# Seven block products for eight in the projections of a recurrent layer and a gated delta layer

## The reference, cut to what matters

```python
def rglru_block(h, in_w, ...):                       # layer 1
    proj = h @ in_w                                  # 1024x1024 @ 1024x2048
    xb, zg = proj[..., :D_RNN], proj[..., D_RNN:]
    xb = causal_dwconv(xb, conv_w) + conv_b
    gates = sigmoid(xb per block @ gate_w + gate_b)
    a_t, b_t from the gates; hseq = scan(a_t, b_t)
    return (hseq * silu(zg)) @ out_w

def gated_deltanet_block(h, in_w, ...):              # layer 2
    proj = h @ in_w                                  # q, k, v, z: 4 x 1024 columns, and 16 more
    qkv = silu(causal_dwconv(proj[..., :o1], conv_w))
    q, k normalised; chunked gated delta rule per head, 8 heads of 128
    return (rms-normed o * silu(z)) @ out_w

x = x + gate * out                                   # after each of the two
```

## Time and profile before

| | |
|---|---|
| median of 3 runs | 2334.98 us (2333.48 to 2340.04) |
| the profiled execution | 2349.8 us |
| its span, first to last instruction | 2348.1 us |
| mean granted TensorE clock | 0.988 |
| PE busy | 2269.5 us, 97% |
| DVE busy | 1205.7 us, 51% |
| ACT busy | 542.0 us, 23% |
| POOL busy | 95.9 us, 4% |

### The profile page before, as it was taken

One profiled execution on the slowest core, in us unless ns is written; L12 is line 12 of the kernel. 1 busy time (PEld: TensorE's weight loads), 2 busy tenths in 40 slices (PEclk: granted clock), 3 DMA queues, 4 the chain that ended last, 5 costly groups with the idle time before them and its releaser, 6 DMA issues. The chain is left out here.

```text
span 2348.1 us, 20195 instructions
## 1 busy us (share of the span) xinstructions
PE 2269.5 (97%) x7290; PEld 1159.0 (49%) x7290; DVE 1205.7 (51%) x1712; ACT 542.0 (23%) x860; POOL 95.9 (4%) x79
## 2 busy tenths in 40 slices
PE   6999999999999999999999998999999999999999
PEld 5444444346656556556554454544444444444443
DVE  4666533253563653644722587347469998341112
ACT  4334422222332332332312510031100000230011
POOL 0000000110101101101010000000000000000000
PEclk8999999999999999999999999899999999999999
DMA  8332310021101101101120224231111111115001
GB/s 313 109 131 86 110 46 0 1 52 45 34 20 40 42 20 40 42 18 43 47 37 18 100 55 73 54 93 33 41 40 41 36 32 45 31 41 188 18 27 45
DMA packets 197709, 134.28 MB, mean 57 GB/s; under 512 B 49868, under 2 KB 171777, under 8 KB 197633
## 3 DMA queue, kind: packets, MB, share of 16 engines
q1 hardware_dynamic: 187825, 131.82, 19.5%
q10 hardware_dynamic: 9440, 0.59, 0.3%
q0 software_dynamic: 384, 1.05, 0.2%
HBM read 118.06 MB, written 14.19 MB: 56 GB/s over the span
## 5 line engine op out<-in xcount | busy, mean ns | idle before, releaser
L1701 PE MATMUL bank<-hT,ring 128*128 128x512 f32 x1472 | 637.3, 594 | 2.6 <-DMA ring<-in_w_in 2.6
L986 PE MATMUL bank<-hT,ring 128*128 128x512 f32 x992 | 461.4, 594 | 0.0
L1701 PEld LDWEIGHTS bank<-hT,ring 128*128 128x128 f32 x1472 | 280.1, 191 | 352.5 <-issue 349.0
L2319 DVE SCALAR_TENSOR_TENSOR yT<-s_arena,yT 128x1024 f32<-128x1024 f32 x240 | 308.3, 1285 | 8.4
L986 PEld LDWEIGHTS bank<-hT,ring 128*128 128x128 f32 x992 | 172.5, 191 | 136.0 <-issue 136.0
L478 PE MATMUL bank<-hT,ring 128*128 128x512 f32 x448 | 194.9, 593 | 0.0
L478 PEld LDWEIGHTS bank<-hT,ring 128*128 128x128 f32 x448 | 85.0, 190 | 105.0 <-issue 104.6
L1701 PE MATMUL bank<-yT,ring 128*128 128x512 f32 x256 | 110.0, 593 | 0.0
L1929 PE MATMUL bank<-resid,s_arena 128*128 128x512 f32 x256 | 110.0, 593 | 0.0
L1437 DVE SCALAR_TENSOR_TENSOR memory<-memory,col_exp_last,bank 128x128 f32<-128x128 f32 x64 | 22.3, 348 | 162.5 <-PE bank L1109 162.5
L1701 PE MATMUL bank<-ssm_y,ring 128*128 128x512 f32 x192 | 83.9, 593 | 0.6 <-DVE s_arena L2333 0.6
(11 more groups left out here) (449 smaller groups left out, 2621.4 us busy)
## 6 DMA issues: line engine op xcount, KB each, us to landing
ring<-in_w_in SPq DMA_DIRECT2D x48, 512.0 KB, 3.9
ada<-in_ada_w SPq DMA_DIRECT2D x8, 2048.0 KB, 7.9
ring<-in_gdn_in_w SPq DMA_DIRECT2D x32, 512.0 KB, 4.8
ring<-in_lru_in_w SPq DMA_DIRECT2D x16, 512.0 KB, 7.0
lru_arena<-in_ada_w SPq DMA_DIRECT2D x6, 1024.0 KB, 12.9
resid<-in_x SPq DMA_DIRECT2D x4, 1024.0 KB, 8.2
decayT<-g_scratch SPq DMA_DIRECT2D x8, 512.0 KB, 4.2
x_scratch<-resid SPq DMA_DIRECT2D x8, 512.0 KB, 6.4
```

The lines of the kernel that those rows point to most:

```text
L986: last = nc.tensor.matmul(bank[:, 2 * (b % 2) + n, :], ring[:, b, k, :], hT[:, k, n * HALF:(n + 1) * HALF], start=(k == 0), stop=(k == KT ...
L1701: last = nc.tensor.matmul(bank[:, 2 * PAIR[name] + h, :], w[:, k, :], src[:, k, h * HALF:(h + 1) * HALF], start=(k == 0), stop=(k == kt - 1))
L2319: dve_b.mark(dve.scalar_tensor_tensor(out=yT[:, n, :], in0=padded[:, p, j:j + S], scalar=taps[:, p, j:j + 1], in1=yT[:, n, :], op0=ALU.mul ...
```

## The change

A product of 2x2 blocks is made with seven block products for eight (the form of Strassen's method by Winograd). The "columns" of the block matrix are the two halves of k, the "rows" are a pair of weight tiles (x and z of a column in the recurrent layer; q with k, and v with z, in the delta layer), and the tokens are cut in two halves of 512. A block product is 4 matmuls of 128x512.

- **Sums of tokens**: T1, T2, T3 (128x2048 each) are made once per layer by DVE and kept in `resid`; T4 takes the place of a quarter of `hT`.
- **Sums of weights**: S1 to S4 (128x512 each) for every pair. In the recurrent layer DVE makes them, one column ahead; in the delta layer POOL does, those of pair b (v, z) behind `rel`, those of pair a (q, k) behind the level masks.
- **Products** are accumulated in two PSUM banks one upon another: P1, P1+P6, then P7 and P4 on top. Between them ACT keeps a copy of the partial sum (`keep`, 128x512 from PSUM to `resid`), and DVE adds it to a bank later (`part`, `join`).
- In the recurrent layer this holds for columns 2 to 7; columns 0 and 1 stay. z is now gated with one function (Silu) in two halves on ACT, and the weighing of a chunk of `ada_w` comes one column later. The order within a column is new on PE, ACT and DVE. x is loaded again into `resid` (4 x 1 MB) before it is added.
- In the delta layer it holds for the projections of heads 1 to 7; head 0 stays. The residual is stored to DRAM at the start of the stage (2 x 2 MB) and loaded again in the last head, between the loads of `out_w`. PE draws 56 instead of 64 in a head: 13 for 15 behind `v_flip`, and none behind `new` in chunks 2 to 7.

```diff
+                    for n in range(FAST, KT):
+                        if n > FAST:
+                            dve_a.wait(pe, f"C11_{n - 1}")
+                        product(n, 1, "A12", B21, f"x{n}", True, True)
+                        gates(n - 1)
+                        dve_a.wait(pe, f"S1_{n}")
...
+                        product(n, 2, "S1", T1, f"P5_{n}", True)
+                        dve_a.wait(pe, f"S2_{n}")
+                        act_a.wait(pe, f"kept0_{n}")
+                        product(n, sums_bank(n), "S2", T2, f"P6_{n}")
+                        dve_a.wait(pe, f"S4_{n}")
+                        act_a.wait(pe, f"kept2_{n}")
+                        product(n, 2, "S4", B22, f"P3_{n}", last_one=True)
+                        act_a.wait(pe, f"kept1_{n}")
+                        product(n, sums_bank(n), "S3", T3, f"P7_{n}")
+                        for j in weighed_in[n]:
                             later(j, n)
+                        if n < KT - 1:
+                            begin_column(n + 1)
+                        dve_a.wait(pe, f"C22_{n}")
+                        product(n, sums_bank(n), "A22", T4, f"z{n}", last_one=True)
+                    gates(KT - 1)
```

The same pair of products in the delta layer, on PE (pair a; pair b is alike, and its P1 and P2 come before a's P4):

```diff
+                        yield from product("a", 0, "A11", tok11, "P1", first=True)
+                        px_dve.wait(pe, "C11b", h, back=1)
+                        yield from product("a", 1, "A12", tok21, "P2", first=True, only=True)
...
+                        yield from product("a", 2, "S1", tok_sum1, "P5", first=True)
+                        sums["a"].wait(pe, "S2", h)
+                        tok_sums.wait(pe, "T2")
+                        px_act.wait(pe, "kept0a", h)
+                        yield from product("a", 0, "S2", tok_sum2, "P6")
+                        sums["a"].wait(pe, "S4", h)
+                        px_act.wait(pe, "kept2a", h)
+                        yield from product("a", 2, "S4", tok22, "P3")
+                        px_act.wait(pe, "kept1a", h)
+                        yield from product("a", 0, "S3", tok_sum3, "P7")
...
+                        px_dve.wait(pe, "C22a", h)
+                        tok_sums.wait(pe, "T4")
+                        yield from product("a", 0, "A22", tok_sum4, "P4")
...
-                        fill(15, 30)
+                        fill(13, 30)
...
-                            fill(1, 2)
+                            fill(int(c < 2), 2)
```

On ACT, POOL and DVE of the delta layer:

```diff
+                        if after is not None:
+                            keep(0, "a", h, "P1", "C11")
                         hd_pe.wait(act, "k_flip", h)
...
                         hd_act.mark(act.activation(cq[:, :], cq[:, :], ACT.Silu), "q_silu")
+                        if after is not None:
+                            keep(2, "a", h, "P5", "C22")
+                            keep(1, "a", h, "P6", "C12")
+                            px_act.mark(act.activation(padded[:, 0, PAD:PAD + HALF], bank[:, 1, :], ACT.Copy), "raw")
                         hd_pe.wait(act, "q_flip", h)
...
                             key_silu(after)
-                            take_z(after)
+                            hd_dve.wait(act, "y", h)
+                            px_dve.wait(act, "C22b", h)
+                            px_act.mark(act.activation(silu_z[:, HALF:S], z_raw, ACT.Silu), "zhi")
+                            px_pe.wait(act, "P4b", h)
+                            px_act.mark(act.activation(silu_z[:, 0:HALF], bank[:, 3, :], ACT.Silu), "zlo")
...
+                        done.mark(g.tensor_tensor(w["S3"], w["A11"], w["S1"], ALU.subtract), "S3")
+                        done.mark(g.tensor_tensor(w["S1"], w["S1"], w["A22"], ALU.add), "S1")
+                        done.wait(g, "S1", head - 1)
+                        done.mark(g.tensor_tensor(w["S2"], w["S1"], w["A11"], ALU.subtract), "S2")
+                        done.wait(g, "S2", head - 1)
+                        done.mark(g.tensor_tensor(w["S4"], w["A12"], w["S2"], ALU.subtract), "S4")
...
                         if after is not None:
+                            px_act.wait(dve, "zhi", h, back=1)
+                            join("C22b", z_raw, 3, 2, "P7b", h)
+                            join("C12b", padded[:, 2, PAD + HALF:], 2, 1, "P3b", h)
                             tap(after, 1, 0, "k", ck)
```

And on SP, in the last head:

```diff
                     sp.dma_start(out_w1, out_w[:, 0:7, HALF:D]).then_inc(out_loaded[2], 16)
+                    px_dve.wait(sp, "C12b", HEADS - 2)
+                    for n in range(2):
+                        sp.dma_start(resid[:, 4 * n:4 * n + 4, :], x1_dram[:, 4 * n:4 * n + 4, :]).then_inc(x1_back, 16)
                     sp.dma_start(ring_flat[:, 6 * HALF:8 * HALF], out_w[:, 7, :]).then_inc(out_loaded[3], 16)
```

More of the change, by code:

```diff
@@ new lines, in _, with product @@
+                    for j in weighed_in[0]:
+                        later(j, 1)
+                    dve_a.wait(pe, "sz0")
+                    pe_a.mark(project_column(1, 1), "z1")
+                    def product(n, to, w, v, name, first=False, last_one=False):
+                        w = blocks(n)[w]
+                        for k in range(KB):
+                            last = nc.tensor.matmul(bank[:, to, :], w[:, k, :], v[:, k, :], start=(first and k == 0), stop=(k == KB - 1), skip_group_check=not (first and last_one))
+                        pe_a.mark(last, name)
@@ new lines, in part @@
+                    def part(name, n, out, to, which, product):
+                        pe_a.wait(dve, f"{product}{n}")
+                        act_a.wait(dve, f"kept{which}_{n}")
+                        dve_a.mark(dve.tensor_tensor(out, bank[:, to, :], kept[which], ALU.add), f"{name}_{n}")
+                    for j in range(TAPS4):
+                        tap(0, j)
+                    weigh_later(0)
+                    gate_plain(0)
+                    weigh_later(1)
+                    gate_input(0)
@@ new lines, in _ @@
+                    gate_mult(0)
+                    recur(0)
+                    for j in range(TAPS4):
+                        tap(1, j)
+                    finish(0)
+                    finish(1)
+                    dve_a.mark(dve.tensor_tensor(T1, T4, B11, ALU.subtract), "T1")
+                    dve_a.mark(dve.tensor_tensor(T3, B22, T4, ALU.subtract), "T3")
+                    gate_plain(1)
+                    dve_a.wait(dve, "T1")
+                    dve_a.mark(dve.tensor_tensor(T2, B22, T1, ALU.subtract), "T2")
```

343 lines of the change are left out of this document (285 added, 58 removed).

## The result

The changed kernel takes 2342.07 us, the median of 16 runs (2336.63 to 2349.78). The kernel before, run beside it, takes 2336.4 (16 runs, 2332.63 to 2341.89). The ratio is 1.0026 with a 95% interval of 1.0015 to 1.0037: a loss of 5.7 us, where a gain of 7.3 was forecast, and 0.07 us above the range. Its profiled execution took 2345.05 us (span 2343.3).

What follows compares the result with a forecast made beforehand. PE, busy 2269.5 of 2348.1 us, was taken as the bound, though delta-head fillers sit in others' waits. Recurrent -19.5 and delta +12.2 gave -7.3, so 2327.5 us against the median of 2334.98; range 2308 to 2342.

Steps and rivals of the forecast that it cites:

- Recurrent layer, -19.5: Columns 2 to 7: 28 matmuls for 32 take 20.6 us off PE, nearly all kept; bounds -20.6 and -12.
- Where PE would stand: Delta heads: PE waits 3.0 us before P3 of pair a and 1.6 before the last product; v_flip 2.5 late.
- The sum of an undisturbed head, +0.9: One delta head: Y16 +1.0, chunks -1.4, end +1.3, so nothing of 6.9 us saved comes through; bounds -0.8 and +4.5.
- the 1.1 taken in all: Delta head: DVE loses 1.1 us beside POOL's sums: 0.3 at a small product, little at decay_a, 0.8 at q's taps.
- Head 0, +1: Start of the delta layer: T4, 2.7 us of DVE ahead of head 0's rel, partly shows, costing 1 us.
- The clock, +0.7 a head: Delta heads: PE's clock falls behind the 3.0 us wait, taken as three in ten of 2.4 us; ends 0 and 2.4.
- the 2.60 us without loss: Profile row: behind a PE wait of 2.60 us, 32 records took 14.00 us, as in 13.90, so no clock loss.
- the 12.2 forecast: Delta layer's total cost: 7 x (0.9 for the head + 0.7 for the clock) + 1 for head 0 = +12.2 us.
- 0.24 us won for a filler of 0.858: Chunks 2 to 7 of a delta head: mem still needs ACT's scaling, so each chunk gains only 0.24; six times, -1.4.
- no contention: Rival, delta heads: POOL and DVE don't meet on the path, wait near 2 us, clock never falls; 2315 us; chance 0.26.
- The clock falling in every head: Rival, delta heads: the clock falls each time behind the wait on kept2a, 7 x 1.7 us more; 2339 us; chance 0.20.
- The others: Rivals: clock falls in the chunks, 2399 us (0.07); PE's work alone counts, 2266 (0.05); last head's reload late, 2333 (0.04).

Runs made afterwards that it cites:

- the run of that part alone: Kernel before with only the recurrent layer's part of the change, delta layer as before: 2318.46 us, 18.1 below the kernel before.
- both_waits: Changed kernel with ACT's copy kept2a ahead of q_silu and DVE's additions C12b and C22b inside chunks 5 and 7: 2327.15 us.
- keep_early: Changed kernel with one edit: ACT makes the copy kept2a ahead of q_silu instead of behind it: 2336.28 us.
- pool_late: Changed kernel with one edit: POOL makes pair b's four sums of weights behind the second level mask instead of behind rel: 2328.53 us.
- delta_alone: Kernel before with only the delta layer's part of the change, recurrent layer as before: 2358.89 us, 22.3 above the kernel before.
- joins_in_chunks: Changed kernel with one edit: DVE makes additions C12b and C22b behind delta of chunks 5 and 7, not behind the last chunk: 2335.46 us.
- fill_behind_new: Changed kernel with one edit: in chunks 2 to 7 the one filling matmul is drawn behind new instead of ahead of it: 2320.26 us.
- three_edits: Changed kernel with the edits of keep_early, joins_in_chunks and pool_late together: 2315.60 us.
- four_edits: three_edits with, at the delta heads' start, PE's wait for head 0's z moved to before P5 and DVE's T4 made earlier: 2316.13 us.

## Why the prediction was wrong

Told by its own steps:

- **Recurrent layer, -19.5.** Right: 19.1 in the traces, 18.1 by the run of that part alone. No wait over 1 us on PE in columns 2 to 7.
- **Where PE would stand.** Right: 3.05 us before P3 of pair a (3.0 forecast), 1.47 before the last product (1.6), `v_flip` 2.7 late (2.5), no fall of the clock in the chunks, and a head longer and not shorter by 8 fewer fillers.
- **The sum of an undisturbed head, +0.9.** Too low: it is +1.5 (94.92 less the 1.3 by which `Y16` came later behind the fall at 590 is 93.6, for 92.12). `Y16` is 1.31 late (704.01 - 668.32 = 35.69 for 34.38), not 1.0, because POOL costs DVE 1.4 at two small operations, where I had put 0.3 at one, and 0.1 at `decay_a`, for the 1.1 taken in all; at the taps, where I had put 0.8, it costs nothing outside the first head, since POOL's last sum ends at 677.87, as they begin. So 1.5 for 1.1 is near by luck: it fell on other operations than those named. The chunks bring 0.14 each and not 0.24, so -0.8 for -1.4, and the end costs 1.0 for 1.3. That is 0.6 too little in each of seven heads, 4.2 us. This is the first term of the sum that failed.
- **Head 0, +1.** Too low, and with the wrong cause; this is the largest step that failed. By the part run alone, from PE's first matmul of the delta layer to the first `k_flip` are 61.61 us (412.73 to 474.34) and 63.63 with the change (412.31 to 475.94): +2.0, of it 1.76 a wait for ACT's gating of z that I hadn't listed. And the head behind it takes 3.8 more than an undisturbed one, by T4 and POOL's sums in each other's way and a wait of 4.57 with its fall of the clock. I had let T4 act on that head's `rel` only, as part of the 1. In both_waits, where the clock doesn't fall there, the first head is 1.7 over the others, so of the 3.8 about half is the clock (an estimate).
- **The clock, +0.7 a head.** The term was a little low (5.5 us over the last six heads, for 4.2 by 0.7 each), and half its mechanism was missing: I took falls behind the wait of 3.0 only, and three of the six came behind the wait of 1.47, which I took to be inside another delay and free. I had read from the 2.60 us without loss that a shorter wait is safe; that row follows a stretch of nothing but 128x512 products, and the wait of 1.47 follows eight chunks of small ones. The first heads show that the row wasn't a limit elsewhere either: the clock fell behind a wait of 2.54 us in keep_early. All this is of one traced execution for each kernel; how often the clock falls in the other executions of the median isn't known.

So the delta layer costs 21.9 in the traces for the 12.2 forecast: 4.2 in the sum of a head, 4.8 at the first head and ahead of it, the rest in the clock. With 1.4 less from the recurrent layer in the medians that is most of the 13 us between -7.3 and +5.7. Of the rivals, no contention is refuted by pool_late. The clock falling in every head, with 2339 us, is what came nearest: it fell in six of seven, if not always where that rival said. I had given it 0.20. Its number is near by luck, since it put 2.4 us in each head, and the last six heads lost 5.5 in all. The others didn't happen. The range was also narrower than its own terms: with all of POOL's 4.7 the sum of a head was bounded by +4.5, which gives some 2353 us, and the range ended at 2342.

What the prediction didn't see at all is the largest number of this study: which of a chunk's two fillers is taken away is worth 22 to 24 us. I had computed "0.24 us won for a filler of 0.858" from the wait behind `new` and didn't ask whether the filler that stayed stood in the chain.

## What to carry to other kernels

Work taken off an engine that fills its waits with it brings only what the chain leaves, so ask of each filler that stays whether it stands between a ready input and the operation that needs it; taking one out may call for moving the other. A copy or an addition for a cheaper product costs least in a queue where its engine already stands idle (behind `delta` on DVE, ahead of `q_silu` on ACT), and most in front of the link that ends the loop. Where two waits can each let the clock fall, look at both: with either one left three of six heads still had a fall, with both gone none.

## What the runs showed of the hardware

- **The clock falls behind a wait of one length in some heads and not in others.** Over the four kernels that have the wait of 2.8 to 3.1 us before P3 in six heads each (the changed one, delta_alone, joins_in_chunks, fill_behind_new), the granted clock fell behind 12 of 24, in otherwise equal heads. Behind the wait of 1.47 us after the chunks (35 in five kernels) it fell behind 10. In fill_behind_new, where the chunks are shorter, it fell there in none of 7; but six of these heads had their fall behind P3, and in 12 of the 13 heads with such a fall none followed behind P4, so the shorter chunks needn't be the cause. In the first head it fell behind those of 4.5 each time (4 of 4) and behind 2.54 and 2.72 (keep_early, pool_late), but not behind 2.51 (both_waits). Behind the waits of 0.9 to 1.9 at other places of these seven heads it never fell.
- **POOL and DVE slow each other**, not one the other: 0.17 us became 0.90 on DVE, and 1.27 became 3.32 on POOL beside a DVE addition of 3.25. In the rows above an operation that comes while the other engine is at work ends with or behind the other's, so a short one can lose several times its own length.
- **A difference of 3 us between two traces may not be found in the medians** (three_edits and four_edits), whose intervals are as wide as that.
